# One decoder step on one core: ten lines of hand-written order moved in the queues of three engines

## The reference, cut to what matters

```
z = x @ w_in                      # q, k, v, u and two gates; x: 264 tokens x 2048
attn = rms_norm(softmax(q k1) - lam * softmax(q k2)) @ v     # 8 heads, two maps each;
                                  # samples read 16 pages of cached keys and values each
x_t = abar * x_(t-1) + B u_t;  y = C x_t + d * u;  g = gelu(y)
ssm = g * sigmoid(g @ w_glu)
merged = gate_a * (attn @ w_proj_attn) + gate_s * (ssm @ w_proj_ssm)
h = layer_norm(alpha * x + merged @ w_out)
y = layer_norm(alpha * h + conv_ffn(h))
```

## Time and profile before

| what | us |
|---|---|
| median of three runs | 1624.69 (1624.34 to 1625.53) |
| the profiled execution | 1625.53 |
| its span, first to last instruction | 1623.4 |
| TensorE busy | 1612.8 |
| VectorE busy | 1146.2 |
| ScalarE busy | 687.6 |
| GpSimd busy | 434.6 |

### The profile page before, as it was taken

How to read it: one execution, slowest core, us unless ns; L and a number is a source line. 1 busy time by engine, 2 the same in 40 slices (tenths; PEclk the granted TensorE clock), 3 DMA queues, 4 the chain that set the end, 5 groups by cost and what they waited for, 6 DMA issues and landing times.

```text
span 1623.4 us, 31564 instructions
## 1 busy us (share of the span) xinstructions
PE 1612.8 (99%) x11816; PEld 1453.6 (90%) x11816; DVE 1146.2 (71%) x1792; ACT 687.6 (42%) x1053; POOL 434.6 (27%) x387
## 2 busy tenths in 40 slices
PE   8999999999999999999999999999999999999998
PEld 7988777777777776999999999999999999999998
DVE  4783987987987953876778977677777776555463
ACT  4311343443443323433546844444444444334353
POOL 1075787787787620000008400000000000000000
PEclk9999999999999999999999999999999999999999
DMA  9689899999999989766665675766666675766662
GB/s 256 209 297 310 307 392 398 382 394 396 389 392 392 371 288 272 185 176 190 175 182 152 182 194 154 206 177 182 181 180 183 166 197 146 206 184 177 188 179 70
DMA packets 472391, 391.87 MB, mean 241 GB/s; under 512 B 23654, under 2 KB 436355, under 8 KB 472276
## 3 DMA queue, kind: packets, MB, share of 16 engines
q1 hardware_dynamic: 401628, 323.33, 64.5%
q10 hardware_dynamic: 70656, 67.11, 12.7%
HBM read 385.30 MB, written 5.46 MB: 241 GB/s over the span
## 4 chain that ended last, share of the span: by engine, by line
PE 97%; DMA 1%; SPq 1%; ACT 1%; issue 0%; ACTq 0%
PE bank L845 27%; PE bank L1246 19%; PE bank L1247 19%; PE bank L1254 19%; PE bank L825 4%; PE bank L993 1%; PE bank L792 1%; PE bank L1019 1%; PE bank L1004 1%; PE bank L874 1%; PE bank L884 1%; PE bank L875 1%; DMA work<-in_cache_v 1%; DMA small<-in_ssm_log_dt 0%; SPq L463 0%; PE bank L1045 0%
## 5 line engine op out<-in xcount | busy, mean ns | idle before, releaser
L1689 ACT ACTIVATE weights_hi<-weight_ring 128x2048 fp32r<-128x2048 f32 (+1 forms) x166 | 309.7, 1866 | 457.1 <-PE bank L1247 323.9
L845 PE MATMUL bank<-work,weight_ring 128*128 128x264 f32 x1920 | 453.9, 391 | 0.0
L2231 DVE TENSOR_TENSOR weights_lo<-weight_ring,weights_hi 128x2048 fp32r<-128x2048 f32 (+1 forms) x166 | 371.1, 2236 | 104.2 <-ACT weights_hi L1689 70.0
L845 PEld LDWEIGHTS bank<-work,weight_ring 128*128 128x128 f32 x1920 | 356.5, 190 | 77.1 <-issue 20.9
L713 POOL TENSOR_TENSOR work<-work 128x512 f32<-128x512 f32 x256 | 319.3, 1277 | 86.9 <-DMA work<-in_cache_k 72.3
L1246 PE MATMUL bank<-h_hi,weights_hi 128*128 128x264 f32 x1184 | 291.6, 285 | 0.0
L1247 PE MATMUL bank<-h_lo,weights_hi 128*128 128x264 f32 x1184 | 290.9, 285 | 0.0
L1246 PEld LDWEIGHTS bank<-h_hi,weights_hi 128*128 128x128 f32 x1184 | 223.4, 189 | 0.0
L1247 PEld LDWEIGHTS bank<-h_lo,weights_hi 128*128 128x128 f32 x1184 | 223.1, 188 | 0.0
L2064 DVE TENSOR_REDUCE work<-work 128x8 f32<-128x512 f32 x256 | 163.4, 676 | 33.2 <-POOL work L713 33.2
L1246 PE MATMUL bank<-hidden_hi,weights_hi 128*128 128x264 f32 x688 | 169.6, 285 | 0.0
(11 more groups left out here) (333 smaller groups left out, 2376.2 us busy)
## 6 DMA issues: line engine op xcount, KB each, us to landing
weight_ring<-in_w_up SPq DMA_DIRECT2D x86, 1024.0 KB, 5.6
work<-in_cache_k SPq DMA_DIRECT2D x128, 512.0 KB, 7.8
work<-in_cache_v SPq DMA_DIRECT2D x128, 512.0 KB, 7.6
weight_ring<-in_w_in ACTq DMA_DIRECT2D x60, 1024.0 KB, 13.8
weight_ring<-in_w_down SPq DMA_DIRECT2D x32, 1024.0 KB, 6.1
weight_ring<-in_w_out SPq DMA_DIRECT2D x16, 1024.0 KB, 5.9
weight_ring<-in_w_down SPq DMA_DIRECT2D x16, 704.0 KB, 4.8
weight_ring<-in_w_proj_attn SPq DMA_DIRECT2D x16, 512.0 KB, 4.2
```

Of the source, the lines that this page charges most:

```text
L845: last = pe.matmul(bank[(n + m) % 2][:, 0:N], chunk_weight(g, k - c * per, m), tiles[k], start=(k == 0), stop=(k == len(tiles) - 1))
L1689: act.activation(w_hi[:, (j % 2) * KT * P:(j % 2) * KT * P + k_tiles * P].bitcast(F32R), slot3(j, 0, k_tiles).rearrange("p k m -> p (k m)" ...
L2231: dve.tensor_tensor(w_lo[:, cols].bitcast(F32R), slot3(off % SLOTS, 0, k_tiles).rearrange("p k m -> p (k m)"), w_hi[:, cols], ALU.subtract ...
```

## The change

It is only an order. No instruction is added and none is taken away. `cx(0, 2)` and `cx(0, 3)` go from the middle of a pair of m-tiles to the place before it. `prompt_pv(H - 2)` goes ahead of `scores(H - 1, 1, 0)`. Three posts in the last pair of gates go to other steps, and ScalarE's queue around them is put in another order. On VectorE `y_out(0)` moves ahead by two pages, the samples' new states go behind `map_weights` and page 11, and `shift(B - 1)` goes ahead of the last step of gelu.

```
 PE      z_tile(("k", 2), ("k", 3))
-        z_group((("k", 4), ("k", 5)), {4: lambda: (cx(0, 2), cx(0, 3))})
+        cx(0, 2)
+        cx(0, 3)
+        z_tile(("k", 4), ("k", 5))
...
+        prompt_pv(H - 2)
         pe.wait_ge(cs_read, 1)
         scores(H - 1, 1, 0)
-        prompt_pv(H - 2)
...
-        {1: combine(B - 1), 2: states_out, 3: sample_states_out, 5: sample_mean_square}
+        {1: combine(B - 1), 4: sample_mean_square, 5: states_out, 7: sample_states_out}

 ACT     combined(B - 1)
+        wait w_ready B + 1; Square (sq_ready); wait ms_done 5; Sqrt (root_ready)
         take(("prompt_states", 0)); copy
+        evict(("g", 30))
         take(("sample_states", 0)); copy
...
         high(0, 0, True)
-        wait w_ready B + 1; Square (sq_ready); wait ms_done 5; Sqrt (root_ready)
-        evict(("g", 30))
         evict(("g", 31))

 DVE     states(0, 3, lambda: reduce_page(0, 5))
-        reduce_pages(0, 6, 7, 8, 9)
+        reduce_pages(0, 6, 7)
         y_out(0)
-        reduce_pages(0, 10, 11, 12, 13, 14, 15)
+        reduce_pages(0, 8, 9, 10, 11, 12, 13, 14, 15)
...
         reduce_page(b, 10)
+        map_weights(i)
+        reduce_page(b, 11)
         if i == H - 2: wait bs_done; xs_new = bank 4 + ax0   (xn_ready)
-        map_weights(i)
-        reduce_page(b, 11)
...
         gelu_t = gelu_t * yg
+        shift(B - 1)
         yg = (gelu_t + 1) * yg
-        shift(B - 1)
         maxima(H - 1, 1)
```

More of the change, by code:

```diff
@@ L1235, in _ @@
             z_group((("g", 30), ("g", 31)),
-                    {1: lambda: combine(B - 1), 2: states_out, 3: sample_states_out, 5: sample_mean_square})
+                    {1: lambda: combine(B - 1), 4: sample_mean_square, 5: states_out, 7: sample_states_out})
             def products(m, off, sums, width=N, between=None):
@@ L1676, in _ @@
             combined(B - 1)
+            act.wait_ge(w_ready, B + 1)
+            act.activation(sq_sample.rearrange("p (h b) -> p h b", h=H), att3[:, :, T:N], ACT.Square).then_inc(sq_ready, 1)
+            act.wait_ge(ms_done, 5)
+            act.activation(root_sample, bank[5][:, 0:H * B], ACT.Sqrt, bias=small[:, 5:6]).then_inc(root_ready, 1)
             take(("prompt_states", 0))
             copy(xf_rows[0:PAIRS, :], bank[2][0:PAIRS, 0:2 * P]).then_inc(mail_read, 1)
+            evict(("g", 30))
             take(("sample_states", 0))
```

## The result

The changed kernel takes 1633.19 us, the median of five runs (1632.0 to 1635.4), beside 1624.69 us for the kernel before. The ratio is 1.0056, with a 95% interval of 1.0043 to 1.0069: slower, by 8.5 us between the medians and by 9.1 us by the ratio, where 6.4 us were forecast. The range of the prediction ended at 1633.5: the median lies 0.3 us inside it, the time by the ratio, 1633.8, 0.3 us beyond. The profiled execution took 1634.26 us with a span of 1632.1 us, 8.7 us more than before.

What follows compares the result with a forecast made beforehand. TensorE, busy 1612.8 of 1623.4 us, was taken as the bound. Its new waits, 2.8 + 0.8 + 0.6 + 0.4 + 1.8 = 6.4 us, gave a median of 1631.1 us, with a range of 1629.0 to 1633.5.

Steps and rivals of the forecast that it cites:

- The bound and the direction: Whole kernel: TensorE is the bound, busy 1612.8 of 1623.4 us; added waits make it slower, chance 0.90.
- Rival (a): At the moved cx, the transfers' slack absorbs the first stall of 2.8 us, giving 1628.3; chance 0.1.
- (c): Rival: not slower, as engines' inputs come sooner than the one execution shows; 1627.5, within 0.2%; chance 0.06.
- (d): Rival: faster, the new order frees TensorE of waits it has; over 0.2% only from waits counted busy; chance 0.02.
- The cx term: At moved cx(0, 3), TensorE waits from 111.6 to 114.4 us for VectorE's states(0, 3): +2.8 us, bounds 2.6 to 3.0.
- My case: Main forecast: TensorE's new waits add up to 6.4 us with the clock staying at 1.00, giving 1631.1 us.
- rival (b): The clock falls in the 2.8 us hole at the moved cx, costing 1.6 us more: 1632.7; chance 0.15.
- `cx(0, 2)` takes half of 1.06 us: At the moved cx: cx(0, 2) starts at 111.05 us, so cx(0, 3) is up at 111.6 us.
- Nothing in the change lets VectorE get there sooner: At the moved cx: VectorE's scan states(0, 3) still ends at 114.35 us, with the same work ahead in its queue.
- y_out costs nothing at its new place: VectorE's y_out(0), two pages earlier: c_done is there by page 7 and its next reader comes next round; no cost.
- The samples' states: Before sample_cx(0): VectorE's addition, behind map_weights and two half pages, is late for TensorE: +0.8 us, bounds 0.7 to 1.7.
- prompt_pv, shift and the last gates: TensorE waits for ScalarE's key-row copy, for maxima, and around the last gates up to projection 0: +0.6, +0.4, +1.8 us.

Runs made afterwards that it cites:

- a: Kernel before with only cx(0, 2) and cx(0, 3) moved ahead of the pair k4/k5; 1629.84 us, ratio 1.0028.
- j: Kernel before with both cx moved ahead of the pair and the first also waiting for the last scan, so they run together; 1630.73 us, ratio 1.0034.
- n: Changed kernel with 10 extra matmuls of ones as filler between its two cx; 1634.62 us, ratio 1.0067.
- d: Kernel before with both cx moved and, on VectorE, the scan's last part ahead of pages 3 and 4; 1626.79 us, ratio 1.0006.
- i: Kernel before with both cx moved and 10 extra matmuls of ones as filler between them; 1631.03 us, ratio 1.0040.
- k: Kernel before with the two cx one step apart inside the pair k4/k5, with no wait; 1625.71 us, ratio 1.0007.
- b: Changed kernel with only the two cx put back in their old places; 1631.50 us, ratio 1.0040.
- m: Changed kernel with both cx and y_out put back, leaving the four later edits; 1628.37 us, ratio 1.0030.
- f: Kernel before with only map_weights and page 11 put ahead of the samples' new states; 1625.51 us, ratio 1.0006.
- c: Kernel before with both cx moved and 20 extra matmuls of ones as filler between them; 1631.47 us, ratio 1.0042.

## Why the prediction was right in direction and too small

**The bound and the direction** held. No moved instruction freed TensorE of a wait, and every input that came late added at least its length. Rival (a), that the transfers' slack eats the stall, fell: a is slower by 0.28% with that move alone. So did (c) and (d).

**The cx term is the step that failed**, 2.8 forecast and 7.5 measured, in three places.

1. My case kept the clock at 1.00 through the hole, and rival (b) happened. A hole of 3.95 us took the clock to 0.50, and so did one of 3.61 (j). The hole in a was only 2.2 us and did so too, while 1.79 (n), 1.16 (d) and 0.90 (i) did not. The Trainium skill, "TensorE: Matmul & The Clock Gate", section "Why this matters for your kernels", asks for no gap of more than about 3 us; a's 2.2 us is a measurement against that figure, and a forecast by it would have left the clock out even with the true hole of a. The price was 2.5 us after, where the clock was low for 6.8 us, and 1.4 to 1.7 in a and j, where it was low for 3.4, near the 1.6 that the start's rows gave. I had the size, and gave the case 0.15.
2. "`cx(0, 2)` takes half of 1.06 us" is wrong. The two write different groups of 32 output columns and ran beside each other: eight records in 1.00 us, four in 0.98 (k). Apart they cost 1.0 us more. The same section of the Trainium skill states that small matmuls with outputs in distinct groups of 32 partitions run concurrently; the trace agrees, with a factor of 1.96 for two, and the group of the earlier trace rows with its eight records in one stretch should have been read with that in mind.
3. "Nothing in the change lets VectorE get there sooner" was right, but I took TensorE's arrival from one execution. The scan hangs on GpSimd's pages and TensorE on its own front, so the hole is not a constant: 2.2 in a, 3.95 after. The execution that I read had the longest front of all, which put TensorE's arrival 1.4 us later than after.

**y_out costs nothing at its new place**: true with the early `cx`, where VectorE does not wait for it. Without the early `cx` VectorE idles 2.40 us (b), and whether that costs TensorE anything is open. b is slower than before by 6.5 us between medians, and m, without the edit, by 3.8; their intervals overlap, so that the runs don't decide it.

**The samples' states**: 0.8 forecast, 0 after, 0.55 alone (f), 0.2 to 0.3 in b and m, 0.8 in n. The term hangs on whether VectorE's small operation meets a GpSimd product, as the working said, but on an operation further ahead in the queue than the one I had priced. That the term came out at nothing made up for 0.8 us of the `cx` term in the sum; this was luck.

**prompt_pv, shift and the last gates**: 0.6, 0.4 and 1.8 forecast; 0.74, 0.50 and 1.97 in the kernel after, and the same alone. The waits are at the lines named, and the two parts of the last one are 1.0 and 0.8. (651.15 + 5.56 is 656.71 and not 656.65, which gives the 1.0.)

**The sum.** 7.5 + 0 + 0.74 + 0.50 + 1.97 = 10.7 between marks; less 2.0 of what the change doesn't own (1.47 of front, 0.45 of waits in the middle, 0.15 and -0.07 elsewhere) it is the 8.7 of the span. The pieces alone give 4.87 + 0.74 + 0.82 + 0.50 + 1.97 = 8.9.

**What stays open.** Keeping the clock up with filler (c, i, n) did not make the runs faster than a or after, although the stretches in the profiles are 0.2 to 2.2 us shorter or, for c, 0.8 longer. One profile of each can't tell whether other executions had the same holes, but each run's mean granted clock tells a part. Three of the ten executions of a have 1.000, so that the clock hardly fell in them, and took 1626.54, 1628.16 and 1630.35 us. Two of the five of n have 1.000 too, and took 1634.15 and 1634.62, no less than after. So the 2.5 us of low clock are shown in the profile of after, and not as a share of the runs' 8.5. The filled kernels are also the only ones that are over 0.1 us longer behind projection 0 (0.3, 0.5 and 0.6 us), for a reason that is not shown. Whether VectorE's idle time in b leads to the late weights was not tried by itself.

## What to carry to other kernels

A wait put into an in-order queue of the bounding engine can cost more than its length: add the low clock behind it (1.4 to 2.5 us here, behind holes of 2.2 to 4.0 us) and the overlap that neighbouring small matmuls lose. Ask which chain the input hangs on. Where it is another one than that of the waiting engine, the hole is a range over executions, not the difference of two times of one trace. When runs spread by more than the term that is asked for, compare stretches between fixed marks, and leave the verdict to the runs of the sum.

## What the runs showed of the hardware

TensorE's granted clock fell from 1.00 to 0.50 with an idle stretch of 2.2 us in the middle of the kernel, and idle stretches of 0.90, 1.16 and 1.79 us at the same place left it at 1.00. What decides between 1.79 and 2.2 was not tried; each of these is one profile, and two of the three short stretches had matmuls of ones ahead of them. The fall came 2.4 us into the idle stretch after, at its end in a, and 1.1 us behind its end in j, and the clock was low for 6.8 us after and 3.4 in a and j. Small VectorE operations that met a GpSimd product ended at about its end: 1.44 us for one of 128x256 that took 0.34 us otherwise (f, n, after), 1.18 us for one of 128x2 in m that took 0.34 to 0.62 in f, after and n. VectorE's sums of 128x512 next to such products did not: two took 1.27 us in f as they did elsewhere.
